# Input halves in sixteen transfers, and the conv taps and modulation sums moved on VectorE, in the attention stage of a hybrid decoder layer

## The reference

```
mod = silu(c) @ w_ada + b_ada            # six vectors of 1024
u   = x * (1 + sc1) + sh1
cb, cc, cx, q, k, v, ga, gb = split(u @ w_in)
y_a = (cb * causal_dwconv(cc * cx, w_conv)) @ w_a      # three taps
z   = q @ k.T / 8                         # 8 heads of 64, blocks of 128 queries
log1m   = where(mask, log_sigmoid(-z), 0)
between = reverse_cumsum(log1m) - log1m
o   = where(mask, exp(log_sigmoid(z) + between), 0) @ v    # stick-breaking attention
mix = (sigmoid(ga) * y_a + sigmoid(gb) * (o @ w_b)) @ w_o
```

## Time and profile before

| | us |
|---|---|
| three timed runs | 2876.31, 2882.66, 2883.45 (median 2882.66) |
| profiled execution | 2877.65, its span 2875.0 |
| PE busy | 2528.3 (88%), mean granted clock 0.937 |
| DVE, ACT, POOL busy | 1525.5 (53%), 1115.9 (39%), 872.4 (30%) |
| `mixer` | from about 333 to 1451 of the span |
| issue to landing, median: block of u, 4096 KB | 17.9 |
| raw weights of a unit, 512 KB / modulation weights, 256 KB | 6.9 / 5.4 |

### The profile page before, as it was taken

One profiled execution on the slowest core, in us unless ns is written; L12 is line 12 of the kernel. 1 busy time (PEld: TensorE's weight loads), 2 busy tenths in 40 slices (PEclk: granted clock), 3 DMA queues, 4 the chain that ended last, 5 costly groups with the idle time before them and its releaser, 6 DMA issues. The chain is left out here.

```text
span 2875.0 us, 37140 instructions
## 1 busy us (share of the span) xinstructions
PE 2528.3 (88%) x12564; PEld 2105.0 (73%) x12565; DVE 1525.5 (53%) x2163; ACT 1115.9 (39%) x1815; POOL 872.4 (30%) x740
## 2 busy tenths in 40 slices
PE   4999789899999999999969969993998999999950
PEld 3888668777888788888857747782887888887840
DVE  4211156665665556565642248884546545526628
ACT  2211145554454445454520012221556545527612
POOL 1111144442222222232202235654222222223327
PEclk7999899999999999999989989995999999999975
DMA  6655676767566664647455554333667656637735
GB/s 239 250 189 188 189 259 207 222 211 236 171 191 200 215 202 150 206 151 210 139 190 175 163 191 132 127 126 132 198 188 238 206 146 181 207 61 241 216 75 224
DMA packets 245962, 534.85 MB, mean 186 GB/s; under 512 B 22436, under 2 KB 92184, under 8 KB 243800
## 3 DMA queue, kind: packets, MB, share of 16 engines
q1 hardware_dynamic: 223256, 468.39, 49.4%
q0 software_dynamic: 15248, 46.62, 7.5%
q10 hardware_dynamic: 7344, 18.35, 1.7%
HBM read 380.26 MB, written 153.02 MB: 185 GB/s over the span
## 5 line engine op out<-in xcount | busy, mean ns | idle before, releaser
L89 PE MATMUL mx_acc<-u_u,mx_w_hi 128*128 128x512 f32 x1792 | 572.6, 401 | 10.2 <-DMA mx_w_lo<-halves 10.2
L605 POOL TENSOR_TENSOR mx_wt<-mx_wt,mx_rest 128x127 f32<-128x127 f32 (+15 forms) x128 | 271.4, 2120 | 715.5 <-DVE mx_rest L810 715.5
L89 PEld LDWEIGHTS mx_acc<-u_u,mx_w_hi 128*128 128x128 f32 x1792 | 326.9, 190 | 75.2 <-DMA mx_w_lo<-halves 10.9
L818 DVE TENSOR_TENSOR mx_wt_lo<-mx_p_t,mx_wt_hi 128x512 fp32r<-128x512 f32 (+2 forms) x320 | 192.2, 605 | 350.9 <-ACT mx_wt_hi L771 349.1
L89 PE MATMUL mx_acc<-u_u,mx_w_lo 128*128 128x512 f32 x896 | 354.4, 396 | 0.0
L771 ACT ACTIVATE mx_wt_hi<-mx_p_t 128x512 fp32r<-128x512 f32 (+2 forms) x320 | 170.6, 533 | 413.2 <-PE mx_p_t L659 366.3
L810 DVE TENSOR_TENSOR_SCAN mx_rest<-mx_rest,mx_zero 128x128 f32<-128x128 f32 (+15 forms) x128 | 319.2, 2494 | 13.9 <-ACT mx_wt L753 13.9
L89 PE MATMUL moe_p_gu<-moe_gu_hi,moe_x_hi 128*128 128x512 f32 x656 | 262.9, 401 | 16.4 <-DVE moe_gu_lo L1770 16.4
L89 PE MATMUL moe_p_gu<-moe_gu_hi,moe_x_lo 128*128 128x512 f32 x656 | 258.5, 394 | 0.0
L89 PE MATMUL moe_p_gu<-moe_gu_lo,moe_x_hi 128*128 128x512 f32 x656 | 258.4, 394 | 0.0
L659 PE MATMUL mx_p_t<-keep_ident,mx_wt 128*128 128x128 f32 x1088 | 176.6, 278 | 46.1 <-POOL mx_wt L605 37.6
(11 more groups left out here) (241 smaller groups left out, 5270.4 us busy)
## 6 DMA issues: line engine op xcount, KB each, us to landing
mx_w_hi<-halves SPq DMA_DIRECT2D x84, 512.0 KB, 3.9
mx_w_lo<-halves SPq DMA_DIRECT2D x84, 512.0 KB, 5.3
moe_gu_raw<-in_w_gate SPq DMA_DIRECT2D x64, 512.0 KB, 5.6
moe_gu_raw<-in_w_up SPq DMA_DIRECT2D x64, 512.0 KB, 6.7
moe_dn_raw<-in_w_down SPq DMA_DIRECT2D x32, 1024.0 KB, 6.9
u_saved<-u_u SPq DMA_DIRECT2D x4, 4096.0 KB, 16.5
u_u<-u_saved SPq DMA_DIRECT2D x4, 4096.0 KB, 17.9
mx_w_mod<-in_w_ada SPq DMA_DIRECT2D x64, 256.0 KB, 5.4
```

The source lines that it names most:

```text
L89: mm = pe.matmul(out, a, b, start=first and n == 0, stop=last and n == len(pairs) - 1, skip_group_check=True)
L605: pool.tensor_tensor(wt[:, t % 2, 0:w - 1], wt[:, t % 2, 0:w - 1], rest[:, t % 2, 1:w], ALU.mult).then_inc(m["weights_done"], 1)
L818: dve.tensor_tensor(wt_lo[:, first:first + k - j], p_t[:, n % TR, 0:(k - j) * P].rearrange("p (j t) -> p j t", t=P), f32(wt_hi[:, first:fi ...
```

## The change

The block of u is loaded in 16 pieces of 256 KB, one per step from step 4 of the even head on (steps 4 to 15, then 0 to 3 of the odd head); the semaphore counts that PE waits for follow. On DVE, `out_unit` keeps only what frees the PSUM bank; the carry copy and the taps are in `taps`, called one group later, behind that group's low half, scan and output. The modulation sum goes from the end of an even step to the first group of the odd step, behind the scan.

```diff
+    U_FROM, U_COUNTS = 4, (16, 2 * KD * 16, 2 * KD * 16 + 16, 4 * KD * 16)
...
-            def load_u(tb):
-                sp.dma_start(f32(u[:, tb % 2]).rearrange("p a k n -> p (a k n)"), u_saved[tb]).then_inc(u_in[tb % 2], 16)
+            def load_u(tb, i):
+                if i == 0 and tb >= 2:
+                    sp.wait_ge(m["filled"], (tb - 1) * TB_UNITS)
+                half, k = divmod(i, KD)
+                sp.dma_start(f32(u[:, tb % 2, half, k]), u_saved[tb][:, i * NB:(i + 1) * NB]).then_inc(u_in[tb % 2], 16)
...
-            load_u(1)
...
-                        if r == 0 and t == 3 and h in (2, 4):
-                            sp.wait_ge(m["filled"], h // 2 * TB_UNITS)
-                            load_u(h // 2 + 1)
+                        i = h % 2 * NT + t - U_FROM
+                        if r == 0 and h < HEADS - 2 and 0 <= i < 2 * KD:
+                            load_u(h // 2 + 1, i)
...
-                            pe.wait_ge(u_in[tb % 2], 16 * (tb // 2) + 16)
+                            pe.wait_ge(u_in[tb % 2], U_COUNTS[tb])
...
+            def taps(n):
+                j = place(n)[1]
+                if KINDS[n] == "cc":
+                    i = kind_no("cc", n)
                     dve.wait_ge(m["carry_step"], 2 * i + 1)
                     dve.wait_ge(m["dve_out"], outs(False, n + 1))
                     dve.tensor_copy(carry[:, j], gated[:, NB:NB + 2]).then_inc(m["carry_step"], 1)
...
+            def earlier(h, slot):
+
+                return (h, slot - 1) if slot > 0 else (h - 1, NS - 1)
...
+                            if t % 2 == 1:
+                                add_mod(h * KD + t // 2)
+                        ha, last = earlier(h, GR_BEFORE[t] + r)
+                        for n in ended(ha, last) if ha >= 0 else []:
+                            taps(n)
                         for n in ended(h, GR_BEFORE[t] + r):
                             out_unit(n)
-                    if t % 2 == 0:
-                        add_mod(h * KD + t // 2)
```

More of the change, by code:

```diff
@@ L843, in out_unit @@
                     dve.tensor_tensor(gated[:, 2:NB + 2], acc[:, n % 2], cx[:], ALU.mult).then_inc(m["dve_out"], 1)
+                elif KINDS[n] == "cb":
+                    i = kind_no("cb", n)
+                    dve.wait_ge(m["filled"], n + 1)
+                    dve.wait_ge(m["conv_step"], 3 * i + 3)
+                    past(dve, c_stored[i % 2], 16 * (i // 2))
+                    dve.tensor_tensor(c_out[:, i % 2], acc[:, n % 2], conv[:], ALU.mult).then_inc(m["dve_out"], 1)
+            def taps(n):
+                j = place(n)[1]
+                if KINDS[n] == "cc":
+                    i = kind_no("cc", n)
                     dve.wait_ge(m["carry_step"], 2 * i + 1)
@@ L854, in out_unit @@
                                                  op0=ALU.mult, op1=ALU.add).then_inc(m["conv_step"], 1)
[L855 to L860, removed]
             def add_mod(n):
```

## The result

The changed kernel takes 2894.76 us (median of 6 runs, 2891.35 to 2897.0), the kernel before 2879.32 (6 runs, 2876.31 to 2883.45): a ratio of 1.0055, 95% interval 1.0043 to 1.0066. It is slower by about 15 us, and near the 2892 us that were forecast. The profiled execution took 2891.35 us, its span 2888.2 us.

The account below looks back on a forecast made before the run. TensorE's waits in the attention stage were taken to bound the kernel. Terms -11.0, -13.5, +20.9, +5.2, +2.3, -2.4, -0.3 and +10 summed to +11 us, giving 2892 us from the middle of the timed runs; range 2872 to 2903.

Parts of the forecast that it names:

- Heads 2 and 4, -13.5: TensorE's waits for halves queued behind the big transfer, and the slower clock behind them, go: -7.1 and -6.4 us.
- Head 0, -11.0: Without the big transfer at the stage's start, unit 2's raw weights land earlier; TensorE's wait shrinks from 11.8 to 0.8 us.
- The transfers together, -24.5: The gain in heads 0, 2 and 4 from replacing the big transfers of input halves by pieces: -24.5 us.
- Step 12, +20.9: Moved taps, held by GpSimd's weighting, delay the second low half: +2.65 us a head, +2.5 in heads 0 and 1.
- The clock, +10: Behind step 12's 3.2 us wait TensorE runs at half clock: 1.7 us, heads 1 to 7, six of seven cases.
- The sums, +5.2: In step 13 the moved modulation sum delays the second low half: +0.65 us a head, 5.2 in all.
- the early part, +2.3 and less: Steps 0 to 8, moved taps and sums: +2.3 us over heads 2 to 7, -2.4 in head 1, -0.3 in head 0.
- The port: Two-input VectorE instructions on SBUF, and the carry copy, wait for GpSimd's whole operation; a sum ahead delays weighting by 0.43 us.
- The clock holds: Rival: the 3.2 us waits in step 12 bring no slow stretch; about 2883 us, no change; chance 22%.
- The taps aren't held, faster: Rival: in step 12 copy and taps get the port within the weighting; -27 us, so 2854; chance 14%.
- The pieces collide: Rival: 48 more issues delay raw weights on the queue in heads 0 and 1; 2903 us; chance 11%.
- The transfers weren't the cause: Rival: raw weights come as late as before, so the first -11 us goes; 2903 us; chance 3%.

Follow-up runs that it names:

- one late transfer each: The pieces-only kernel with each block of input halves in one 4 MB transfer again, issued in step 4 of heads 0, 2 and 4; 2865.48 us.
- order only: The changed kernel with the input halves in one transfer per block as before, VectorE's new order kept; 2913.15 us, ratio 1.0110.
- pieces and taps: The changed kernel with the modulation sums back at the ends of even steps; 2890.27 us, ratio 1.0027.
- pieces only: The changed kernel with VectorE's order of the kernel before, taps and sums at their old places; 2857.78 us, ratio 0.9917.
- pieces and sums: The changed kernel with the taps back behind the unit's product; 2867.84 us, ratio 0.9950.
- Copy on ScalarE: The changed kernel with the two-element carry copy done by ScalarE instead of VectorE; 2890.94 us, ratio 1.0036.
- port free: The changed kernel with GpSimd's weighting of steps 5 and 13 left out beyond 128 columns; 2881.50 us, stage 1097.1 us.

## Why the prediction was right

- *Heads 2 and 4, -13.5.* Right: moving those two transfers gave 13.4 us of stage. My reason, halves queued behind the block, fits what one late transfer each shows. The size of 256 KB, from which I argued that a piece hides, mattered little: 1 MB did as well, and most came with the move to step 4 in one piece.
- *Head 0, -11.0.* The mechanism was right, the size 2 us too large: 8.8 in the trace after, 9.8 with the transfer alone. I had the raw weights landing near 358; ScalarE went on at 364.25, since the k, v and q loads and the stores stand ahead of it without the big transfer as well, and the store ahead took 5.68 us to issue. And of the 9.8 only 3.7 reached the stage's end when the other two transfers stayed. I had let early gains add up to the end; later waits of heads 0 to 4 took more than half back.
- *The transfers together, -24.5.* Beside the old order they gave 24.1 us of time and 19.9 of stage; beside the new order (order only against after) 18.4 of stage.
- *Step 12, +20.9.* Right to a tenth in heads 2 to 7: waits of 3.19 where 0.52 + 2.65 = 3.17 stood, carry copy 2.62 us ending with the weighting. In heads 0 and 1 the wait was 4.96 us, where 2.1 + 2.5 = 4.6 was forecast. One sum of the working does not add up as written: 1281.84 + 0.40 + 0.51 + 1.46 is 1284.21, while 1283.75, from which +2.65 follows, needs 1.91 us between the copy's end and the low half. The trace after has 1.88 (1287.77 to 1289.65), so the result was right and the 0.40 was one term too many.
- *The clock, +10.* Right, though the chance of six in seven and the 1.7 us had single cases behind them. A head of pieces and taps takes 136.4 us from step 12 to step 12 against 131.8 in pieces only: +4.6, of which 2.67 are the wait, 0.4 the steps up to 12, and 1.5 the matmuls at 1.2 GHz behind the wait, up to the first group of step 13; over the eight heads these are 9.4 us. Taps and clock together were 31 by the prediction and 29.9 by the runs.
- *The sums, +5.2, and the early part, +2.3 and less.* Step 13 was right: 0.67 us a head in heads 2 to 7 of pieces and sums, where 0.65 stood; in the trace after, its wait of 0.50 us shows in heads 5 and 6. The weightings grew by the 0.43 us forecast. The early part was right in the trace after for heads 5 to 7, +0.39 each against pieces only, and 0.4 to 0.7 in heads 2 to 4. Undersized was what the sums do in the crowded heads: 11.9 us alone, 6.5 beside the taps.
- *The sum, +11.* The stage grew by 16.6 us, the time by 15.4. VectorE's order alone made the stage 35.0 us longer, where the terms for it add up to 35.7; transfers that gave 18.4 instead of 24.5 are the term that was too large. That 2892 stood within 3 us of the median is in part luck: +11 was 4 us short, and it was added to 2881, 1.7 us above the median before.
- *The port.* The prediction spoke of two-input instructions and of the copy. Copy on ScalarE shows that a one-input TENSOR_SCALAR on SBUF is held as well; L832 and L835, which read PSUM, ran their 0.43 and 0.42 us beside the weighting as usual. The Trainium skill, page "SBUF — State Buffer", section "Who interferes with whom", has both: `copy`, `cast` and `tensor_scalar` can enter the modes that use two ports and so contend for the shared pair, and a VectorE instruction with at most one SBUF input, outside those modes, does not contend. The traces agree, with 2.62 and 2.88 us for the held and 0.43 and 0.42 for the others.
- *The rivals.* The clock holds: it fell behind the new wait in all eight heads of the trace after, and held in single cases of copy on ScalarE only (last section). For this rival I had cited the wait of 2.13 us in head 1, behind which it held; the same trace has one of 2.10 us in head 0, at 460.10, behind which a pair of matmuls takes 1.06 us. So the length of the wait alone did not decide it. The taps aren't held, faster: refuted by the row of 2.62 us, and port free shows what it would have been, a stage of 1097.1 us, even with the sums where the change put them. The pieces collide: TensorE's wait at head 1's start is 1.6 us longer after, 0.9 in pieces only; not 10 us. The transfers weren't the cause: refuted by pieces only.

## What to carry to other kernels

Here work moved "behind the scan" landed exactly where the engine that shares VectorE's port begins one of its longest instructions; price such a move by that instruction's remaining time, and look at what VectorE owes TensorE next behind it. Cut such work into pieces and put each behind the instruction that somebody waits for: the same taps cost 30 us in one block in step 12, came out even at step 4 (won in one head, lost in six), and gained 8 us when spread. When a change joins two edits, run each alone: here one was worth -24 us and hid inside a result of +15.

## What the runs showed of the hardware that was not expected

The same wait does not always bring the slow clock. In copy on ScalarE TensorE waits 3.06 us in step 12 of each of heads 2 to 7. Behind the one in head 3, then behind the one in head 4, the same instructions:

```profile
881.03 0.47 PE L662 MATMUL mx_p_t<-keep_ident,mx_wt 128*128 128x128 f32 x1 [3.06 <-DVE mx_wt_lo L829]
...
882.05 1.16 PE L89 MATMUL mx_acc<-u_u,mx_w_hi 128*128 128x512 f32 x2
...
883.44 1.05 PE L89 MATMUL mx_acc<-u_u,mx_w_hi 128*128 128x512 f32 x2
...
1018.47 0.33 PE L662 MATMUL mx_p_t<-keep_ident,mx_wt 128*128 128x128 f32 x1 [3.06 <-DVE mx_wt_lo L829]
...
1019.05 0.67 PE L89 MATMUL mx_acc<-u_u,mx_w_hi 128*128 128x512 f32 x2
...
1019.80 0.62 PE L89 MATMUL mx_acc<-u_u,mx_w_hi 128*128 128x512 f32 x2
```

Head 3 runs at 1.2 GHz for a while and takes 137.4 us to the next such group; head 4 keeps 2.4 GHz and takes 135.3. Heads 2, 5 and 6 fell to 1.2 GHz as head 3 did, head 7 held as head 4. From this group to the fourth of step 13 the two that held take 12.2 us and the others 13.6 to 14.4, so the price of one slow stretch is 1.3 to 2.1 us here. Whether a wait of this size brings one differs from case to case; what decides it, these runs do not show.

A copy of two elements a partition can cost most of the length of the other engine's instruction: 0.15 us with the port free, 0.81 beside the short weighting of step 5, 2.62 beside the weighting of 3.36 us in step 12.
